# Who asks for the down weights of an expert round: SyncE's queue or ScalarE's

## The chip, the core and the metric

The kernel runs on one core of one Trainium2 chip. The metric is the device time of one execution in microseconds (us). Three executions of the kernel before took 2102.54, 2100.34 and 2096.74 us; the median is 2100.34 us.

## What is computed

A trunk of two layers on 1024 tokens of 1024 channels in float32: a token mixer (layer 0 a gated one, layer 1 a pooling one), and after each a mixture of experts. In the mixture a router picks two of 32 experts for each token, and each expert is a gated pair of matrices and a down matrix:

```
def expert_block(args):
    xb, e = args                                   # 128 token rows, one expert
    hid = jax.nn.silu(xb @ w_gate[e]) * (xb @ w_up[e])   # 1024 -> 512
    return hid @ w_down[e]                               # 512 -> 1024
```

2048 pairs of a token and an expert are cut into blocks of at most 128 rows of one expert. The results go back to their tokens, weighted and added.

## The kernel before

**Items and rounds.** One block of one expert is an item. There are n items in a layer (n is found on the device, and every engine reads it from a small table in SBUF). Round i computes gate and up of item i (on TensorE: 8 weight chunks of 128 x 1024, the helper `gate_up`), then transposes the rows of item i+1 (`x_transposes`, line 850), then down of item i-1 (4 chunks, `down`), then transposes item i's hidden rows (line 888). So a round eats 12 chunks of 512 KB: units 0 to 7 (gate and up, `GU`) and 8 to 11 (down, `DN`).

**How a chunk gets to TensorE.** It lands in one of 12 raw slots (8 in `big`, 4 in `raw`; `moe_raw`). ScalarE rounds it into `w_hi` (`unit`, recorded at line 1025), VectorE subtracts that from the raw chunk into `w_lo` (line 1420), and TensorE multiplies three times for each pair of tiles (hi x hi, hi x lo, lo x hi: lines 619 to 621). `w_hi` and `w_lo` are rings of 4 slots: ScalarE may write the `w_hi` slot of a unit only when TensorE is done with the unit four before (the wait on `M.used` in `unit`, line 1227). VectorE waits for `M.hi`, TensorE for `M.lo`. `M.lo` also tells that the raw slot is free, since VectorE reads it last.

**ScalarE's round** (`round_`, lines 1261 to 1272): units 0 to 3, two copies of the finished rows out of PSUM (`y_out`, line 1248), the split of the hidden rows (`h_split`), units 4 to 7, SiLU (line 1240), units 8 to 11, and at the end the split of the next item's rows, two copies (`x_split`). VectorE's round follows it: units 0 to 3, `h_split`, units 4 to 11, the product `hidden` (line 1792), `x_split`. ScalarE, VectorE, TensorE, GpSimd and SyncE each have a loop of their own over the rounds, with an index register; ScalarE's loop starts at line 1308.

**Who asks for the chunks.** SyncE, on its DMA queue, in a loop over i from 4 to n-1 (lines 403 to 411): it reads two expert numbers from the table, then for j = 0 to 7 waits until unit j of round i-1 is through VectorE and asks for gate or up chunk j of item i (`load_gu`, recorded at line 341), then for j = 0 to 3 waits for unit 8+j of round i-1 and asks for down chunk j of item i-1 (`load_dn`, line 345), which round i uses. After the loop SyncE asks for the last item's four down chunks into other slots (lines 412 to 414), and in layer 0 for weights of the next stage (lines 417 to 420). GpSimd gathers and scatters the token rows on a queue of its own.

The lines on which the change works:

```
with sp.Fori(4, n) as i:                       # 403
    e_up = sp.value_load(table[... i ...])     # 404
    e_dn = sp.value_load(table[... i - 1 ...]) # 405
    for j in range(GU):                        # 406
        sp.wait_ge(M.lo, ROUND * (i - 1) + j + 1)
        load_gu(e_up, j)
    for j in range(DN):                        # 409
        sp.wait_ge(M.lo, ROUND * (i - 1) + GU + j + 1)
        load_dn(e_dn, j)
```

Of the kernel before, what the change touches and what calls it, by code (L numbers as in the profile page):

```python
# [18 lines left out]
P = 128  # L19
# [10 lines left out]
E = 32  # L30
# [6 lines left out]
GU, DN = 8, 4  # L37
ROUND = GU + DN
# [24 lines left out]
def encoder_trunk(nc, A, out):  # L63
    ctx = ExitStack()
    with ctx:
        def sb(name, shape, dt):
            return ctx.enter_context(nc.sbuf_tensor(name, shape, dt))
# [30 lines left out]
        table = sb("table", [1, 2, TABLE], I32)  # L98
# [60 lines left out]
        moe_raw = [bu[:, n * UNIT:(n + 1) * UNIT] for n in range(GU)] + [raw[:, n, :] for n in range(DN)]  # L159
# [114 lines left out]
        def _(sp):  # L274
# [58 lines left out]
            def moe(L, next_weights):  # L333
                M = m[L]
# [4 lines left out]
                def load_gu(e, j, slots=moe_raw):  # L339
                    w = gate if j < DN else up  # L340
                    sp.dma_start(slots[j].rearrange("p (e k f) -> p e k f", e=1, k=2),
                                 w[:, bass.ds(e, 1), j % DN, :, :]).then_inc(M.raw[j], 16)

                def load_dn(e, j, slot=None, landed=None):
                    sp.dma_start((slot if slot is not None else moe_raw[GU + j]).rearrange("p (e k d) -> p e k d", e=1, k=1),
                                 down[:, bass.ds(e, 1), j:j + 1, :]) \
                        .then_inc(landed if landed is not None else M.raw[GU + j], 16)
# [54 lines left out]
                n = sp.value_load(table[0:1, 0, TABLE - 1:TABLE], min_val=E - 2, max_val=ITEMS_MAX - 2) + 2  # L402
                with sp.Fori(4, n) as i:
                    e_up = sp.value_load(table[0:1, 0, bass.ds(i, 1)], min_val=0, max_val=E - 1)
                    e_dn = sp.value_load(table[0:1, 0, bass.ds(i - 1, 1)], min_val=0, max_val=E - 1)
                    for j in range(GU):
                        sp.wait_ge(M.lo, ROUND * (i - 1) + j + 1)
                        load_gu(e_up, j)
                    for j in range(DN):
                        sp.wait_ge(M.lo, ROUND * (i - 1) + GU + j + 1)  # L410
                        load_dn(e_dn, j)
                e_dn = sp.value_load(table[0:1, 0, bass.ds(n - 1, 1)], min_val=0, max_val=E - 1)
                for j in range(DN):
                    load_dn(e_dn, j, early_raw[j], g.last_dn)
# [32 lines left out]

            sp.sem_inc(q.lo, RING)
            moe(0, pool_first)


# [13 lines left out]
            for hf in range(HALVES):  # L465
                pool_out(hf, HALVES * PV + hf * PO)
            moe(1, lambda n: None)


# [553 lines left out]
        def _(act):  # L1023
# [186 lines left out]
            def moe(L, wait_y, wait_tile):  # L1210

                M, n1 = m[L], 4 * L + 3
# [11 lines left out]
                def unit(c, loads, used, gap=0, slots=moe_raw):  # L1224
                    act.wait_ge(M.raw[c], 16 * loads)
                    if used is not None:
                        act.wait_ge(M.used, used)
                    copy(w_hi[:, c % RING, :], slots[c]).then_inc(M.hi, 1 + gap)

                def x_split(i, dst=x_hi):  # L1230
                    for b in range(2):
                        act.wait_ge(M.x_full, 2 * i + b + 1)
                        copy(dst[:, 4 * b:4 * b + 4, :].rearrange("p k t -> p (k t)"), bank[4 + b][:, :]) \
                            .then_inc(M.x_hi, 1)

                def silu(i):
                    act.wait_ge(M.used, ROUND * i + DN)
                    if L == 0 and isinstance(i, int) and i == 0:
                        act.wait_ge(g.fold_stored, 16 * 2)
                    nc.scalar.activation(silu_g, bank[0][:, :], ACT.Silu).then_inc(M.silu, 1)  # L1240

                def h_split(i, dst=h_hi):
                    act.wait_ge(M.h_full, i + 1)
                    copy(dst.rearrange("p k t -> p (k t)"), bank[6][:, :]).then_inc(M.h_hi, 1)
# [6 lines left out]
                def y_out(i, used):  # L1251
                    act.wait_ge(M.used, used)
                    act.wait_ge(M.meta_s, i + 1)
                    weighted_rows(y_sb, 2, meta_s)
# [6 lines left out]
                def round_(i, slots, down_slots=moe_raw, following=True):  # L1261
                    for c in range(4):
                        unit(c, i + 1, ROUND * i + c - 3, slots=slots)
                    y_out(i - 2, ROUND * i)
                    h_split(i - 1)
                    for c in range(4, GU):
                        unit(c, i + 1, ROUND * i + c - 3, slots=slots)
                    silu(i)
                    for c in range(GU, ROUND):
                        unit(c, i, ROUND * i + c - 3, slots=down_slots)  # L1270
                    if following:
                        x_split(i + 1)
# [32 lines left out]
                round_(2, moe_raw, early_down)  # L1305
                act.wait_ge(rt.table, L + 1)
                n = act.value_load(table[0:1, 0, TABLE - 1:TABLE], min_val=E - 2, max_val=ITEMS_MAX - 2) + 2
                with act.Fori(3, n - 1) as i:
                    round_(i, moe_raw)
                round_(n - 1, moe_raw, following=False)  # L1310
                end_unit(0, n)
                end_unit(1, n)
# [729 lines left out]
```

## Time and profile before

| what | before |
|---|---|
| median of three executions | 2100.34 us (2096.74 to 2102.54) |
| span of the profiled execution, first to last instruction | 2094.7 us |
| TensorE, busy share of the span | 97% |
| TensorE's granted clock, mean | 0.982 |
| VectorE | 75% |
| ScalarE | 65% |
| DMA, mean over the span | 267 GB/s |
| SyncE's queue (q1), share of 16 engines' span | 64.7% |
| ScalarE's queue (q10) | 1.3% |

Of the profiled execution only the span is recorded, no device time of its own. The median of the three executions stands 5.6 us above that span, the fastest 2.0 us and the slowest 7.8 us. A share is an average over very different stages: the two stages of expert rounds fill about half of the span, and there every engine is far busier than in the rest. So the shares above only say where to look; the rows further down are from one round and from the two stages.

### The profile page before, as it was taken

How to read it: one execution, taken by the hardware profiler on the slowest of the kernel's cores; microseconds unless marked ns; L12 is line 12 of the kernel's file. 1: busy time of each engine (PE TensorE's matmuls, PEld its weight loads, DVE VectorE, ACT ScalarE, POOL GpSimd, SP SyncE). 2: the span in 40 equal slices, each digit the busy share in tenths (PEclk: the TensorE clock that was granted, in tenths of full speed). 3: DMA queues.
4: the chain of work that ended last, by engine and by line, in shares of the span. 5: the costliest groups of instructions: out<-in, count | busy, mean ns of one | idle time of the engine just before them, and what ended most of it. 6: DMA issues, size and time to landing. Idle time of an engine off the chain costs nothing.

```text
span 2094.7 us, 32415 instructions
## 1 busy us (share of the span) xinstructions
PE 2023.5 (97%) x9566; PEld 1677.0 (80%) x9566; DVE 1567.1 (75%) x1878; ACT 1362.9 (65%) x1744; POOL 358.0 (17%) x439
## 2 busy tenths in 40 slices
PE   7999999999998999999999989998799999999996
PEld 6888778888877888888888868887688888888883
DVE  4334453336568999999999986867799999999995
ACT  3452244433447888888888874325588888888884
POOL 1000000000022222222232200001322222222220
PEclk9999999999999999999999989998799999999998
DMA  7232213332459999999999984233889999999996
GB/s 286 92 99 71 82 61 122 102 100 102 160 148 342 357 380 380 388 385 372 383 376 386 393 319 148 91 150 131 275 331 375 382 378 380 376 379 390 392 374 259
DMA packets 166952, 560.15 MB, mean 267 GB/s; under 512 B 31552, under 2 KB 32800, under 8 KB 164848
## 3 DMA queue, kind: packets, MB, share of 16 engines
q1 hardware_dynamic: 138960, 510.72, 64.7%
q0 software_dynamic: 25488, 39.57, 5.5%
q10 hardware_dynamic: 2448, 9.14, 1.3%
q8 instruction: 32, 0.52, 0.1%
q14 instruction: 24, 0.20, 0.0%
HBM read 541.94 MB, written 51.97 MB: 284 GB/s over the span
## 4 chain that ended last, share of the span: by engine, by line
PE 87%; DVE 5%; DMA 5%; ACT 1%; issue 1%; POOL 1%; SPq 0%; POOLq 0%; DVEq 0%; ACTq 0%
PE bank L619 27%; PE bank L621 26%; PE bank L620 26%; PE bank L850 3%; PE bank L699 1%; PE bank L888 1%; DVE big L1428 1%; DMA big<-in_w_up 1%; PE bank L688 1%; DVE big L1678 1%; DVE bank L1674 1%; DMA raw<-in_w_down 1%; DMA big<-normed,metas 1%; PE bank L738 1%; DMA big<-y_rows 1%
## 5 line engine op out<-in xcount | busy, mean ns | idle before, releaser
L619 PE MATMUL bank<-w_hi,a_hi 128*128 128x512 f32 x1944 | 773.1, 398 | 5.1 <-DVE a_lo L1420 2.8
L621 PE MATMUL bank<-w_hi,a_lo 128*128 128x512 f32 x1944 | 760.5, 391 | 0.0
L620 PE MATMUL bank<-w_lo,a_hi 128*128 128x512 f32 x1944 | 758.4, 390 | 0.0
L1420 DVE TENSOR_TENSOR w_lo<-raw,w_hi 128x1024 fp32r<-128x1024 f32 x372 | 454.2, 1225 | 353.4 <-ACT w_hi L1025 328.9
L1025 ACT ACTIVATE w_hi<-raw 128x1024 fp32r<-128x1024 f32 x372 | 392.8, 1060 | 458.2 <-PE bank L621 435.3
L1420 DVE TENSOR_TENSOR w_lo<-big,w_hi 128x1024 fp32r<-128x1024 f32 x530 | 620.1, 1219 | 29.3 <-ACT w_hi L1025 23.7
L1025 ACT ACTIVATE w_hi<-big 128x1024 fp32r<-128x1024 f32 x530 | 549.2, 1063 | 107.1 <-PE bank L621 106.9
L619 PEld LDWEIGHTS bank<-w_hi,a_hi 128*128 128x128 f32 x1944 | 367.1, 189 | 79.5 <-issue 4.2
L621 PEld LDWEIGHTS bank<-w_hi,a_lo 128*128 128x128 f32 x1944 | 366.0, 188 | 79.2
L620 PEld LDWEIGHTS bank<-w_lo,a_hi 128*128 128x128 f32 x1944 | 366.9, 189 | 72.6
L1420 DVE TENSOR_TENSOR a_lo<-bank,a_hi 128x512 fp32r<-128x512 f32 x227 | 147.7, 683 | 39.2 <-ACT a_hi L1025 39.2
L619 PE MATMUL bank<-a_hi,w_hi 128*128 128x512 f32 x384 | 149.7, 390 | 0.0
L621 PE MATMUL bank<-a_hi,w_lo 128*128 128x512 f32 x384 | 149.4, 389 | 0.0
L620 PE MATMUL bank<-a_lo,w_hi 128*128 128x512 f32 x384 | 149.4, 389 | 0.0
L1025 ACT ACTIVATE a_hi<-bank 128x512 fp32r<-128x512 f32 x227 | 125.3, 595 | 36.4 <-PE bank L850 23.8
L570 POOL DMA_INDIRECT y_rows<-big,metas x65 | 66.6, 1024 | 317.6 <-ACT big L1248 303.0
L619 PE MATMUL bank<-w_hi,y_hi 128*128 128x512 f32 x256 | 101.3, 396 | 5.3 <-DVE big L1678 3.6
L621 PE MATMUL bank<-w_hi,y_lo 128*128 128x512 f32 x256 | 100.1, 391 | 0.0
L620 PE MATMUL bank<-w_lo,y_hi 128*128 128x512 f32 x256 | 100.1, 391 | 0.0
L554 POOL COPY metas<-cols 128x4 int32<-128x4 int32 x61 | 65.4, 1072 | 159.7 <-PE bank L850 135.6
L850 PEld LDWEIGHTS bank<-cf,big 128*128 128x128 f32 x520 | 73.4, 206 | 21.4 <-DMA big<-normed,metas 12.4
L850 PE MATMUL bank<-cf,big 128*128 128x128 f32 x520 | 74.4, 287 | 15.8 <-DMA big<-normed,metas 15.8
(199 smaller groups left out, 1707.0 us busy)
## 6 DMA issues: line engine op xcount, KB each, us to landing
big<-in_w_gate SPq DMA_DIRECT2D x260, 512.0 KB, 5.3
big<-in_w_up SPq DMA_DIRECT2D x254, 512.0 KB, 5.7
raw<-in_w_down SPq DMA_DIRECT2D x244, 512.0 KB, 5.7
raw<-in_a_w_in SPq DMA_DIRECT2D x64, 512.0 KB, 3.9
raw<-in_a_w_out SPq DMA_DIRECT2D x32, 512.0 KB, 3.3
big<-y_rows SPq DMA_DIRECT2D x12, 1024.0 KB, 7.4
big<-in_w_down SPq DMA_DIRECT2D x16, 512.0 KB, 7.9
raw<-in_b_w_in SPq DMA_DIRECT2D x16, 512.0 KB, 5.0
```

The source lines that it names most:

```text
L554: nc.gpsimd.tensor_copy(meta_g, ahead_g).then_inc(M.meta_g, 1)
L570: pool.indirect_dma_start(out=y_rows[L][:, :], out_offset=bass.IndirectOffsetOnAxis(ap=meta[:, 1:2], axis=0), in_=rows.rearrange("p n f -> ...
L619: pe.matmul(dst, left_hi, right_hi, start=first, stop=False)
L620: pe.matmul(dst, left_hi, right_lo, start=False, stop=False)
L621: return pe.matmul(dst, left_lo, right_hi, start=False, stop=last)
L688: last = pe.transpose(bank[b + k // 4][:, k % 4 * P:(k % 4 + 1) * P], x_res[:, t, k * P:(k + 1) * P], ident)
L699: last = pe.matmul(bank[b][:, 0:LGC], xt[L][t][:, k * P:(k + 1) * P], router[:, k, :], start=k == 0, stop=k == KC - 1)
L738: last = pe.matmul(bank[c % nb][:, t * P:(t + 1) * P], v_all[:, t, c * P:(c + 1) * P], w_s[:, c * P * HEADS // SGU, :], start=True, stop=True)
L850: last = pe.transpose(bank[4 + k // 4][:, k % 4 * P:(k % 4 + 1) * P], rows[:, k // 2, k % 2, :], ident)
L888: last = pe.transpose(bank[6][:, k * P:(k + 1) * P], cols_of[:, k, :], ident)
L1025: return nc.scalar.activation(dst, src, ACT.Copy)
L1420: return nc.vector.tensor_tensor(dst, src, f32(hi), ALU.subtract)
```

## The change

SyncE's loop loses the read of the second expert number and the four waits and requests for down chunks. ScalarE's loop gets them, behind the whole of its round: at the end of round i it reads the expert number of item i from the table, and for j = 0 to 3 waits until unit 8+j of round i is through VectorE and asks, on ScalarE's own DMA queue, for down chunk j of item i. Slots, sizes, semaphores and the set of transfers are the same. The loops' bounds cover the same items (before: i-1 from 3 to n-2 on SyncE; after: i from 3 to n-2 on ScalarE).

```
                 with sp.Fori(4, n) as i:
                     e_up = sp.value_load(table[0:1, 0, bass.ds(i, 1)], min_val=0, max_val=E - 1)
-                    e_dn = sp.value_load(table[0:1, 0, bass.ds(i - 1, 1)], min_val=0, max_val=E - 1)
                     for j in range(GU):
                         sp.wait_ge(M.lo, ROUND * (i - 1) + j + 1)
                         load_gu(e_up, j)
-                    for j in range(DN):
-                        sp.wait_ge(M.lo, ROUND * (i - 1) + GU + j + 1)
-                        load_dn(e_dn, j)
...
+                down_of = A["w_down"][L].rearrange("e (k p) d -> p e k d", p=P)
                 with act.Fori(3, n - 1) as i:
                     round_(i, moe_raw)
+                    e_dn = act.value_load(table[0:1, 0, bass.ds(i, 1)], min_val=0, max_val=E - 1)
+                    for j in range(DN):
+                        act.wait_ge(M.lo, ROUND * i + GU + j + 1)
+                        act.dma_start(moe_raw[GU + j].rearrange("p (e k d) -> p e k d", e=1, k=1),
+                                      down_of[:, bass.ds(e_dn, 1), j:j + 1, :]).then_inc(M.raw[GU + j], 16)
                 round_(n - 1, moe_raw, following=False)
```

## Rows read from the trace of the kernel before

**Rows 1.** Both stages of expert rounds: busy time, granted clock, DMA share, GB/s.
```profile
core 0: us, PE busy (x) PEld busy (x) DVE busy (x) ACT busy (x) POOL busy (x), PEclk, DMA share, GB/s
680.94:1196.75 515.81, 515.81 (x2436) 430.74 (x2435) 482.43 (x465) 446.66 (x522) 141.70 (x174) 1.00 0.98 380
1527.00:2025.00 498.00, 498.00 (x2352) 415.86 (x2351) 465.88 (x448) 430.98 (x505) 136.10 (x167) 1.00 0.98 378
```

**Rows 2.** Waits in layer 0's rounds, 688.5 to 1192.3 us (none is TensorE's).
```profile
ACT w_hi L1025 <- PE bank L621: 67.6, 226, 0.4
...
DVE a_lo L1420 <- ACT a_hi L1025: 12.1, 29, 0.4
DVE w_lo L1420 <- ACT w_hi L1025: 7.5, 29, 0.3
```

**Rows 3.** Timeline, ScalarE, from unit 11 of one round to unit 10 of the next.
```profile
start us, us, engine line op out<-in xcount [idle before <-releaser]
1105.81 1.06 ACT L1025 ACTIVATE w_hi<-raw 128x1024 fp32r<-128x1024 f32 x1 [0.30 <-PE bank L621]
1106.77 1.07 ACT L1025 ACTIVATE a_hi<-bank 128x512 fp32r<-128x512 f32 x2
1108.13 1.06 ACT L1025 ACTIVATE w_hi<-big 128x1024 fp32r<-128x1024 f32 x1 [0.29 <-PE bank L621]
...
1112.30 1.06 ACT L1025 ACTIVATE w_hi<-big 128x1024 fp32r<-128x1024 f32 x1 [0.36 <-PE bank L621]
...
1114.88 2.97 ACT L1025 ACTIVATE w_hi<-big 128x1024 fp32r<-128x1024 f32 x3
...
1119.59 1.05 ACT L1025 ACTIVATE w_hi<-raw 128x1024 fp32r<-128x1024 f32 x1
1120.86 1.06 ACT L1025 ACTIVATE w_hi<-raw 128x1024 fp32r<-128x1024 f32 x1 [0.23 <-PE bank L621]
1122.22 1.06 ACT L1025 ACTIVATE w_hi<-raw 128x1024 fp32r<-128x1024 f32 x1 [0.30 <-PE bank L621]
```

**Rows 4.** Timeline, VectorE, the same round.
```profile
1105.54 2.58 DVE L1420 TENSOR_TENSOR w_lo<-raw,w_hi 128x1024 fp32r<-128x1024 f32 x2
...
1109.84 4.78 DVE L1420 TENSOR_TENSOR w_lo<-big,w_hi 128x1024 fp32r<-128x1024 f32 x4
```

**Rows 5.** Timeline, TensorE: transposes, down, gate and up, the next round's transposes.
```profile
1105.61 1.11 PE L850 MATMUL bank<-cf,big 128*128 128x128 f32 x8
1106.47 0.47 PE L619 MATMUL bank<-w_hi,a_hi 128*128 128x512 f32 x1
...
1112.39 0.47 PE L619 MATMUL bank<-w_hi,a_hi 128*128 128x512 f32 x1
...
1123.40 1.11 PE L850 MATMUL bank<-cf,big 128*128 128x128 f32 x8
```

**Rows 6.** ScalarE's loop branch: all rounds, then one round; line 1227 behind it.
```profile
L1308 ACTq COMPARE_BRANCH  x57: 40/45/54, 697.4 to 2026.7; - x57
...
L1308 ACTq FUSED_REGOPS  x2: 37/44/50, 1106.8 to 1107.0; - x2
...
L1227 ACTq FUSED_REGOPS  x1: 37/37/37, 1107.1 to 1107.1; - x1
```

**Rows 7.** SyncE's table read and four requests; a wait's sum; ScalarE's table read.
```profile
L412 SPq FUSED_REGOPS  x2: 51/102/152, 1197.8 to 1198.2; - x2
L412 SPq TENSOR_LOAD <-table x1: 276/276/276, 1197.9 to 1197.9; - x1
L412 SPq SEQ_ASSERT  x1: 18/18/18, 1198.4 to 1198.4; - x1
...
L345 SPq FUSED_REGOPS  x4: 37/37/37, 1198.5 to 1200.0; - x4
L345 SPq MOVE big<-in_w_down x4: 29/29/29, 1198.6 to 1200.1; - x4
L345 SPq DMA_DIRECT2D big<-in_w_down x4: 332/332/333, 1198.6 to 1200.2; - x4
...
L410 SPq ALU_OP  x2: 37/37/37, 1105.9 to 1107.3; - x2
...
L1307 ACTq TENSOR_LOAD <-table x1: 466/466/466, 679.6 to 679.6; - x1
```

**Rows 8.** DMA requests on ScalarE's queue: one beside a running activation; the first one.
```profile
554.28 1.06 ACT L1025 ACTIVATE w_hi<-raw 128x1024 fp32r<-128x1024 f32 x1 [2.91 <-PE bank L621]
554.30 0.40 ACTq L1063 DMA_DIRECT2D normed<-big  x1
...
L1119 ACTq DMA_DIRECT2D cf<-in_c_float x1: 432/432/432, 0.9 to 0.9; - x1
```

**Rows 9.** TensorE released by VectorE, across engines.
```profile
1214.84 0.68 DVE L1792 TENSOR_TENSOR big<-bank,big 128x512 f32<-128x512 f32 x1
...
1215.58 0.33 PE L888 MATMUL bank<-cf,big 128*128 128x128 f32 x1 [0.29 <-DVE big L1792]
```

**Rows 10.** SyncE's requests in one round; landing of down chunks, 1100 to 1220 us.
```profile
1111.22 3.89 SPq L341 DMA_DIRECT2D big<-in_w_gate  x4
1117.24 3.74 SPq L341 DMA_DIRECT2D big<-in_w_up  x4
1122.07 4.34 SPq L345 DMA_DIRECT2D raw<-in_w_down  x4
...
DMA to landing us min/median/max: 5.1/5.8/9.2
```

**Rows 11.** TensorE's waits for transfers, whole kernel.
```profile
PE bank L1000 <- DMA big<-y_rows: 5.9, 1, 5.9
...
PE bank L1000 <- DMA raw<-y_rows: 1.0, 1, 1.0
```

**Rows 12.** Two windows inside a round, busiest and barest; columns as in the first group.
```profile
1105.70:1107.20 1.50, 1.50 (x12) 1.42 (x11) 1.36 (x2) 1.40 (x2) 0.16 (x1) 1.00 1.03 418
...
1119.20:1120.70 1.50, 1.50 (x9) 1.23 (x8) 1.45 (x3) 1.44 (x3) 0.00 (x0) 1.00 0.93 348
```

## The prediction

> **What bounds the kernel now.** I read the stages first: in the two stretches of expert rounds TensorE is busy for the whole of 515.81 and 498.00 us at a granted clock of 1.00 (the 2.4 GHz level), VectorE for 94% and ScalarE for 87% [rows 1]. Then the waits of these rounds: TensorE has none, ScalarE waits for TensorE 226 times (67.6 us in 504 us), always to refill the ring of four, and VectorE waits for ScalarE twice a round, for 0.4 and 0.3 us [rows 2]. So the rounds run at TensorE's pace, 17.79 us each (1105.61 to 1123.40, [rows 5]), and neither a transfer nor a queue holds them: nothing can be gained in them, and the question is whether the new work on ScalarE's sequencer stays under TensorE's cover. For that I read one round instruction by instruction on the three engines [rows 3 to 5].
>
> **What the change removes.** SyncE loses a table read and four requests a round. Its gate and up requests still wait for VectorE to free each slot (first request at 1111.22, [rows 10]), so they go out when they did. Worth: nothing.
>
> **What it adds on ScalarE, and when.** ScalarE's sequencer runs ahead of its engine by one pending activation: the loop branch stands at 1106.8, when the first of the two row copies starts at 1106.77 and the second is still to run [rows 3, 6]. The new instructions take the place of that branch, so they begin at 1106.8 and run beside the two copies. That a request runs beside an activation is in the trace: a 0.40 us request at 554.30 inside an activation of 554.28 to 555.34 [rows 8]. The table read: SyncE's, instruction by instruction, 0.051 + 0.276 + 0.152 + 0.018 = 0.50 us, with four gaps of 0.04, 0.66 us (from 1197.8 to 1198.5, [rows 7]). A request: 0.037 + 0.029 + 0.333 with three gaps of 0.04 is 0.52 us, which is the spacing of the four there (1198.6 to 1200.2 for three); the sum for the wait's value adds 0.037 and a gap, so 0.59 us, and four are 2.37 us. The waits themselves: unit 11 goes into VectorE when ScalarE is done with it (1105.81 + 1.06 = 1106.87) and is through at about 1108.12 (1105.54 + 2.58, [rows 4]); the fourth request gets to its wait at about 1106.76 + 0.66 + 3 x 0.59 = 1109.2. So no wait blocks. The last request ends at 1106.76 + 0.66 + 2.37 = 1109.79. The branch and the first wait's sum follow, 0.32 us before (1106.8 to 1107.1, [rows 6]) and 0.08 for the sum itself: ScalarE starts unit 0 of the next round at **1110.19** in place of 1108.13 [rows 3], 2.06 us later.
>
> **What is queued behind it.** Unit 0 is needed by TensorE when gate and up begin; down (24 products) and four transposes lie between, so that is at 1112.37, just ahead of the row at 1112.39 [rows 5]. After its start it takes 1.06 us on ScalarE, 0.03 to VectorE, 1.21 there (4.78 us for four, overlapping a little, [rows 4]) and 0.05 from VectorE's end to TensorE (1214.84 + 0.68 to 1215.58, [rows 9]): 2.36 us. 1110.19 + 2.36 = 1112.55 against 1112.37: TensorE waits 0.18 us. Before, the same unit was ready at 1109.84 + 1.21 + 0.05 = 1111.10, with 1.27 us in hand, and VectorE came to it 0.65 us after ScalarE was done (1109.84 for 1109.19): that cover eats all but a tenth of the 2.06 us. Units 1 to 3 follow at 0.97 us each in place of TensorE's pace, so unit 3 starts at 1113.10 against 1112.30, and y_out, h_split and unit 4 are 0.80 us late. Unit 4 then starts at 1115.68; 1.06 + 0.03 + 1.21 + 0.05 gives 1118.03, where TensorE comes at 1112.37 + 4 x 1.36 = 1117.81, or 1117.99 with the 0.18 (TensorE's time for one unit, by which it spaces ScalarE's units at 1120.86 and 1122.22, [rows 3]): 0.04 more. By unit 9 ScalarE waits for TensorE again: unit 8 at about 1120.0 for 1119.59, unit 9 at 1121.05, which is 1120.86 with TensorE's own delay; VectorE, with 94% busy, gets back to ScalarE's heels by unit 11. So nothing piles up from round to round; what is lost is what TensorE waited, **0.22 us a round**. ScalarE's loop turns 57 times [rows 6]: 57 x 0.22 = 12.5 us. In the same measure: span 2094.7 + 12.5 = 2107.2 us, and the median stands 5.6 us above the span shown, so 2100.3 + 12.5, about 2113, which I round down to 2112 since the gaps are more likely over- than undercounted in 0.04 steps.
>
> **The bounds of that cost.** ScalarE's trace shows no request or table read inside a round. Below: if the sum for the wait costs nothing beside the rest (4 x 0.077 less), the last request ends at 1109.48 and TensorE never waits: 0 us. Above: a request as long as ScalarE's first, 0.432 us [rows 8], adds 0.4, and a table read as long as ScalarE's one so far, 0.466 us [rows 7], adds 0.19: 0.22 + 0.59 = 0.81 us a round, 46 us. I take SyncE's figures because they are the same instructions in a running loop; the first of a kind on an engine is the far row. The Trainium skill (DMA: Bandwidth & Descriptors, Latency and other measured facts) gives a tensor load a floor of about 600 ns. The trace disagrees, with 276 ns for the load alone; by the page the table read would cost 0.32 us more and the change 31 us in all.
>
> **The transfers.** Down chunk 0 is asked for at about 1107.6 in place of 1104.3 (the round before its row at 1122.07, [rows 10]), chunk 3 at 1109.3 in place of 1108.3. Unit 8 reads the first at 1120.0. That is 12.4 us for a landing that took 5.8, 9.2 at most [rows 10]: hidden. SyncE's requests end at 1121 and ScalarE's begin at 1125.3, a pause of 4.4 us that the transfers in flight (5.8 us each to land) about fill; the queues move 380 GB/s on average [rows 1] and 418 at best [rows 12], so 9% of a round, 1.6 us, may stand idle before transfers bind. After the loop SyncE asks for the last down chunks and the next stage's weights some 5 us earlier, while ScalarE's last four wait in their own queue; they have the same 12 us. Nothing.
>
> **The rivals.** *It is hidden after all* (not slower). For it: the shortfall is 0.2 us out of 3.0, and rests on gaps of 0.04 us. It decides at a unit 0 that starts by 1110.0, that is, when table read and requests take less than 2.83 us in place of 3.03. Time 2100, give or take 2. The Trainium skill (DMA: Bandwidth & Descriptors, Issuing engines are not separate DMA queues) says that issuing on several engines only saves sequencer time, and here SyncE's was never short; by that rule this case holds. *The sequencer's work is dearer on ScalarE*: 0.5 to 0.81 us a round, 2129 to 2147. It sits in the same place and decides from requests of 0.40 us each. For it: ScalarE's own first request and read [rows 7, 8]; against: they were the first of their kind. The Trainium skill's floor for a tensor load (same page and section as above) would put the read's share of it at the upper end; no row shows it in a loop. *The transfers fall behind*: if more than 1.6 us a round stood idle, each further 1 us would cost 57 us, 2157; against: 12 us of cover. *Faster*: not in the rounds, as TensorE is full there; only at the ends, where loads go out earlier, and there TensorE's waits for transfers after the rounds are 5.9 + 1.0 us [rows 11], on rows that wait for the scatter and not for weights: 2093 at best.
>
> **How the numbers follow.** Chances: the forecast (0.1 to 0.5 us a round, 2106 to 2129) 0.45; hidden 0.40; dearer 0.09; transfers behind 0.02; faster 0.04. What can be told from no change is 0.3%, 6.3 us, or 0.11 us a round. Slower is 0.45 + 0.09 + 0.02 = 0.56, same 0.40, faster 0.04. The range takes in the hidden case and its scatter (2097) and goes into the dearer one to 0.54 us a round (2131). The likeliest case's own range is 2106 to 2129.
>
> **What would show it.** Right: in the rounds TensorE shows a wait for VectorE's w_lo (line 1420) once a round at the start of gate and up, of about 0.2 us, and rounds of 18.0 us; ScalarE's unit 0 starts 2.0 us later after the second row copy, with units 1 to 3 spaced by 0.97 us; VectorE waits for w_hi at unit 0 for about 1.1 us. Hidden: the same shifts, but no wait of TensorE and 17.79 us. Dearer: requests over 0.4 us or a table load over 0.4 us, and a wait of TensorE of 0.5 us or more. Wrong altogether: rounds longer with ScalarE waiting for a landing of a down chunk, or requests that hold until the activations before them are done, so that unit 0 starts after 1110.5.

## The result, and the profile after

The changed kernel takes **2113.7 us** (median of four runs, 2108.7 to 2117.3), where the kernel before took 2099.3 us in the four runs beside it: slower, at a ratio of 1.0075 (95%: 1.0061 to 1.0089), some 13 to 19 us. The forecast of 2112 us was close. Part of that is luck: two causes of different size add up to it, and the smaller one stood in the prediction at nothing.

All times below are of profiled executions unless a median is named. The one of the changed kernel was the fastest of its four, at 2108.7 us; what the other three lost on top, no trace shows. Its span grew from 2094.7 to 2107.0 us, by 12.3. Measured from one round's row transposes on TensorE to the next, each of the 57 looped rounds took 17.80 us before (17.79 and 17.81 by turns, [rows 5]) and 18.03 us on average after (17.79 to 18.91). That is 13.2 us over all rounds; outside them the changed kernel gained 0.9. The first looped round of each layer begins before the first request on ScalarE and still takes 17.79 us, so it is 55 rounds that carry the loss, 0.24 us each.

The window view over layer 0's rounds in the changed kernel, for the first line of [rows 1] (window, length, busy us of TensorE, its weight loads, VectorE, ScalarE and GpSimd, granted clock, DMA share, GB/s):

```profile
690.00:1195.00 505.00, 504.16 (x2357) 416.89 (x2357) 457.20 (x449) 418.35 (x505) 119.22 (x168) 1.00 0.99 376
```

The clock is still 1.00 (2.4 GHz). TensorE seems as full as before, while VectorE and ScalarE are down from 94% and 87% to 91% and 83%. The rounds' 1.3% are a part of that; the rest is overlap, since instructions that follow one another at once, as units 0 to 3 below, take 3.91 us for four where one alone takes 1.06.

The waits of layer 0's rounds in the changed kernel, which answer to [rows 2] (columns: us in total, times, longest):

```profile
ACT w_hi L1021 <- PE bank L617: 73.4, 81, 2.5
DVE w_lo L1422 <- ACT w_hi L1021: 45.3, 67, 1.6
...
ACT w_hi L1021 <- DMA raw<-in_w_down: 9.3, 11, 1.8
...
PEld bank L615 <- DVE w_lo L1422: 3.4, 13, 0.8
...
PE bank L615 <- DVE w_lo L1422: 0.6, 1, 0.6
```

Three things are to be seen. ScalarE's 226 short waits for its ring have become 81 long ones: it now comes late once a round instead of waiting at each unit. ScalarE waits 11 times for a down chunk to land, which it never did before. And TensorE's own row holds a single wait of 0.6 us, its weight loads another 13 of 3.4 us in all, though 28 of these rounds are longer, by 5.8 us together: most delays of 0.1 to 0.2 us do not show there, and have to be read from start times.

One ordinary round, on the three engines (start, duration):

```profile
732.64 1.07 ACT L1021 ACTIVATE a_hi<-bank 128x512 fp32r<-128x512 f32 x2
733.44 2.13 ACTq L1310 DMA_DIRECT2D raw<-in_w_down  x4
736.00 3.91 ACT L1021 ACTIVATE w_hi<-big 128x1024 fp32r<-128x1024 f32 x4 [2.30 <-PE bank L617]
```

```profile
737.10 3.50 DVE L1422 TENSOR_TENSOR w_lo<-big,w_hi 128x1024 fp32r<-128x1024 f32 x3 [1.31 <-ACT w_hi L1021]
```

```profile
737.91 0.60 PE L884 MATMUL bank<-cf,big 128*128 128x128 f32 x4
738.38 0.50 PE L615 MATMUL bank<-w_hi,a_hi 128*128 128x512 f32 x1
```

This round began at 731.47. The second row copy starts 1.64 us later, at 733.11, as in the kernel before; the four requests stand in the place of the branch of [rows 6], and unit 0 starts at 736.00: 4.53 us into the round, where it was 2.52 before (1108.13 - 1105.61, [rows 3, 5]). It ends at 737.06, VectorE starts on it at 737.10 with no cover left, is done about 1.21 later at 738.31, and TensorE's first gate/up product follows at 738.38. That is 0.47 us behind the transposes of h, where it was 0.35 before (1112.04, then 1112.39), and 6.91 us into the round for 6.79. In layer 0's rounds before, this product came at 6.79 throughout. "PE bank L617" in the bracket of unit 0 names the last semaphore that unit 0 waited for; ScalarE's own requests are what held it up.

Two rounds in which the last down chunk (unit 11) is late, ScalarE alone. The first begins at 1127.65, the second at 1036.70:

```profile
1126.47 1.06 ACT L1021 ACTIVATE w_hi<-raw 128x1024 fp32r<-128x1024 f32 x1 [0.30 <-PE bank L617]
1128.18 1.06 ACT L1021 ACTIVATE w_hi<-raw 128x1024 fp32r<-128x1024 f32 x1 [0.64 <-DMA raw<-in_w_down]
1129.14 0.58 ACT L1021 ACTIVATE a_hi<-bank 128x512 fp32r<-128x512 f32 x1
1129.62 0.36 ACTq L1310 DMA_DIRECT2D raw<-in_w_down  x1
1129.62 0.59 ACT L1021 ACTIVATE a_hi<-bank 128x512 fp32r<-128x512 f32 x1
1130.20 1.61 ACTq L1310 DMA_DIRECT2D raw<-in_w_down  x3
1132.24 3.91 ACT L1021 ACTIVATE w_hi<-big 128x1024 fp32r<-128x1024 f32 x4 [2.02 <-PE bank L617]
```

```profile
1038.35 1.06 ACT L1021 ACTIVATE w_hi<-raw 128x1024 fp32r<-128x1024 f32 x1 [1.75 <-DMA raw<-in_w_down]
1039.32 0.58 ACT L1021 ACTIVATE a_hi<-bank 128x512 fp32r<-128x512 f32 x1
1039.37 0.36 ACTq L1310 DMA_DIRECT2D raw<-in_w_down  x1
1039.80 0.59 ACT L1021 ACTIVATE a_hi<-bank 128x512 fp32r<-128x512 f32 x1
1039.95 1.54 ACTq L1310 DMA_DIRECT2D raw<-in_w_down  x3
```

In the first, unit 11 waits 0.64 us for its down chunk and the row copies behind it are late, but the requests are not: the first goes out 1.97 us into the round (1129.62), as in the ordinary one (733.44 for 731.47). Unit 0 starts at 4.59 because the second request took 0.47 us. In the second, unit 11 waits 1.75 us, the first request goes out only 2.67 us into the round, unit 0 starts at 5.22 (1041.92), and the round takes 18.68 us. The page of the profile shows where the late chunks come from, in its section of transfers (count, KB each, median us from request to landing):

```profile
big<-in_w_gate SPq DMA_DIRECT2D x260, 512.0 KB, 9.0
big<-in_w_up SPq DMA_DIRECT2D x254, 512.0 KB, 10.0
raw<-in_w_down ACTq DMA_DIRECT2D x228, 512.0 KB, 9.1
```

Before, the same three medians were 5.3, 5.7 and 5.7 us.

Laid side by side, the 55 rounds follow two simple sums. The first instruction of the table read starts at the later of two moments, to 0.01 us: 1.15 us into the round, when TensorE has just ended the second four of the row transposes, for which the second row copy waits, and 0.21 us behind the start of unit 11. In 27 rounds unit 11 waits for its chunk, but in only 8 does it start late enough to move the read, and in two of these by no more than 0.07 us. And a round takes 17.80 us plus the start of unit 0 less 4.37 us, to within 0.05 us.

### The profile page after: what moved, and what is told of

It reads as the page before. It is cut to its first block, busy times and chain, and to the rows that moved or that the text cites. A ratio compares the mean times of both kernels' runs of the same rounds, so it can differ in the third digit from the quotient of the medians.

```text
span 2107.0 us, 32418 instructions
## 1 busy us (share of the span) xinstructions
PE 2033.4 (97%) x9566; PEld 1676.1 (80%) x9566; DVE 1548.1 (73%) x1878; ACT 1334.9 (63%) x1745; POOL 320.0 (15%) x439
## 4 chain that ended last, share of the span: by engine, by line
PE 70%; DMA 19%; DVE 5%; issue 2%; ACTq 2%; ACT 2%; POOL 1%; SPq 0%; POOLq 0%; DVEq 0%
PE bank L615 21%; PE bank L617 21%; PE bank L616 21%; DMA raw<-in_w_down 15%; PE bank L846 2%; PE bank L695 1%; ACTq L1310 1%; DVE big L1430 1%; DMA lists<-payload,place 1%; PE bank L884 1%; POOL lists L524 1%; DMA big<-normed,metas 1%; PE bank L684 1%; DVE big L1680 1%; DVE bank L1676 1%
## 5 line engine op out<-in xcount | busy, mean ns | idle before, releaser
L617 PE MATMUL bank<-w_hi,a_lo 128*128 128x512 f32 x1944 | 760.6, 391 | 0.0
L1422 DVE TENSOR_TENSOR w_lo<-raw,w_hi 128x1024 fp32r<-128x1024 f32 x372 | 444.7, 1222 | 357.0 <-ACT w_hi L1021 351.5
L1422 DVE TENSOR_TENSOR w_lo<-big,w_hi 128x1024 fp32r<-128x1024 f32 x530 | 615.7, 1220 | 83.3 <-ACT w_hi L1021 81.7
L1021 ACT ACTIVATE w_hi<-big 128x1024 fp32r<-128x1024 f32 x530 | 521.9, 1055 | 136.6 <-PE bank L617 126.2
L615 PEld LDWEIGHTS bank<-w_hi,a_hi 128*128 128x128 f32 x1944 | 366.8, 189 | 95.9 <-DVE w_lo L1422 12.4
L617 PEld LDWEIGHTS bank<-w_hi,a_lo 128*128 128x128 f32 x1944 | 366.1, 188 | 79.3
L617 PE MATMUL bank<-a_hi,w_lo 128*128 128x512 f32 x384 | 149.6, 390 | 0.0
L617 PE MATMUL bank<-w_hi,y_lo 128*128 128x512 f32 x256 | 100.6, 393 | 0.0
L559 POOL COPY metas<-cols 128x4 int32<-128x4 int32 x63 | 22.3, 354 | 424.3 <-DMA cols<-lists 424.3
```

Source lines behind the costliest of these rows:

```text
L559: nc.gpsimd.tensor_copy(meta_s, ahead_s).then_inc(M.meta_s, 1)
L615: pe.matmul(dst, left_hi, right_hi, start=first, stop=False)
L617: return pe.matmul(dst, left_lo, right_hi, start=False, stop=last)
L1021: return nc.scalar.activation(dst, src, ACT.Copy)
L1422: return nc.vector.tensor_tensor(dst, src, f32(hi), ALU.subtract)
```

## The experiments

Two theories went into them. **S**: ScalarE's sequencer is what costs, with its table read and four requests between the second row copy and unit 0. **T**: the requests for the down chunks come late and in a burst after a pause, the DMA engines run short, and chunks land late.

| kernel | median us | ratio to before, 95% | span | excess of the 57 rounds over 17.80 |
|---|---|---|---|---|
| after | 2113.7 | 1.0061 to 1.0089 | 2107.0 | 13.2 |
| e1_sync_late | 2112.2 | 1.0045 to 1.0089 | 2109.2 | 5.2 |
| e2_read_early | 2106.5 | 1.0029 to 1.0063 | 2104.6 | 6.1 |
| e3_read_twice | 2136.2 | 1.0174 to 1.0208 | 2134.1 | 37.7 |
| e4_spread | 2096.1 | 0.9993 to 1.0012 | 2094.3 | 0 |
| e5_small_requests | 2097.8 | 0.9992 to 1.0011 | 2099.5 | 0 |
| e6_small_full | 2098.3 | 1.0001 to 1.0020 | 2096.4 | 2.0 |
| e7_small_read_twice | 2126.9 | 1.0131 to 1.0165 | 2124.4 | 30.7 |
| e8_sync_pairs | 2095.7 | 0.9988 to 1.0009 | 2091.6 | 0 |
| e9_filled_pause | 2117.4 | 1.0076 to 1.0109 | 2115.6 | 18.5 |
| e10_sync_late_filled | 2120.3 | 1.0090 to 1.0131 | 2117.6 | 12.9 |
| e11_one_held | 2114.9 | 1.0060 to 1.0094 | 2114.1 | 14.6 |
| e12_sync_late_one_held | 2113.2 | 1.0045 to 1.0084 | 2115.0 | 6.9 |

Each kernel's ratio is to the kernel before on the same chip; its medians there were 2096.4 to 2099.3 us (one execution of 10643 us beside e4 and e6 to e8 is left out of the ratios).

### The late burst without ScalarE (e1), the read moved away (e2), the read doubled (e3)

e1 is the kernel before, with one wait ahead of SyncE's four requests:

```
+                    sp.wait_ge(M.lo, ROUND * (i - 1) + GU + DN)
                     for j in range(DN):
-                        sp.wait_ge(M.lo, ROUND * (i - 1) + GU + j + 1)
                         load_dn(e_dn, j)
```

> SyncE keeps the down requests, but waits once for unit 11 to be through VectorE and then asks for all four: the times of the changed kernel's requests (2.7 to 4.2 us after the rows' transposes begin, against 2.0 to 4.0) without anything new on ScalarE. Theory S (the time ScalarE's sequencer needs between the second row copy and unit 0 sets the loss): TensorE never waits, rounds of 17.80 us, 2099 us, even if chunks land later. Theory T (the late burst of requests makes chunks land late, and that sets the loss): down chunks land after 9 us or more, ScalarE waits for some of them, 2103 to 2113 us.

It lost 14 us by the ratio, with nothing new on ScalarE's sequencer. So T is real, against the prediction. But it lost them in another way than the changed kernel. The first 22 rounds of layer 0 take 17.79 or 17.81 us as before; after them single rounds take 0.1 to 0.6 more; and of the 14.5 us by which its span is longer only 5.2 are in the looped rounds. From the end of one layer's looped rounds to the start of the other's it takes 336.8 us, where the kernels whose landings stay short (before, e4 to e8) take 330.6 to 333.1, and behind the second layer's rounds 72.4, where they take 69.2 to 70.0. That late chunks hold up what follows there is likely, but was not followed up. The rest, 1.8 us, lies ahead of the loops, where nothing was changed and those kernels differ among themselves by 5 us. The median landing of a down chunk grows under it. In the window 690 to 800 us, and then in 1020 to 1110 us, in e1:

```profile
raw<-in_w_down SPq DMA_DIRECT2D x24, 512.0 KB, 6.7
...
raw<-in_w_down SPq DMA_DIRECT2D x20, 512.0 KB, 12.5
```

In the changed kernel:

```profile
raw<-in_w_down ACTq DMA_DIRECT2D x24, 512.0 KB, 6.5
...
raw<-in_w_down ACTq DMA_DIRECT2D x20, 512.0 KB, 10.4
```

In the kernel before both windows have a median of 5.5 and 5.4.

e2 is the changed kernel with the table read in another place, behind ScalarE's unit 8:

```
                     for c in range(GU, ROUND):
                         unit(c, i, ROUND * i + c - 3, slots=down_slots)
+                        if read and c == GU:
+                            e_dn = act.value_load(table[0:1, 0, bass.ds(i, 1)], ...)
...
                 with act.Fori(3, n - 1) as i:
-                    round_(i, moe_raw)
-                    e_dn = act.value_load(table[0:1, 0, bass.ds(i, 1)], ...)
+                    e_dn = round_(i, moe_raw, read=True)
```

> The changed kernel with the table read moved up, behind unit 8 of the round, where ScalarE's sequencer is a unit ahead; the four waits and requests stay at the end. Theory S: unit 0 starts 0.66 us earlier than in the changed kernel, about 3.9 us after the rows' transposes begin in place of 4.54; the shortfall was 0.23 us, so TensorE stops waiting and the time is 2099 to 2102 us. Theory T: the requests go out only 0.66 us earlier, still in one burst, so chunks land late as before and the time stays at 2107 to 2113 us.

Unit 0 starts 4.01 us into the round on average, for 4.62 in the changed kernel, and the first gate/up product is back at 6.79 us: the sequencer's cost is gone. Yet 9.7 us by the ratio are left, and 6.1 us of its profile are in single rounds later on, with ScalarE waiting for transfers, as here in layer 0's rounds:

```profile
ACT w_hi L1021 <- DMA big<-in_w_up: 16.1, 13, 2.3
...
ACT w_hi L1021 <- DMA raw<-in_w_down: 6.0, 10, 1.3
```

That is T by itself again, now through ScalarE's queue.

e3 doubles the read in the changed kernel:

```
                     e_dn = act.value_load(table[0:1, 0, bass.ds(i, 1)], ...)
+                    e_dn = act.value_load(table[0:1, 0, bass.ds(i, 1)], ...)
```

> The changed kernel with the table read done twice at its place. Theory S: with the cover used up, every further 0.66 us on ScalarE's sequencer is paid in full in each of the 57 rounds: 38 us more than the changed kernel, 2151 us, rounds of 18.7 us. Theory T: requests 0.66 us later each round; as the transfers in flight fill most of that, 2114 to 2125 us.

The rounds take 18.46 us, 0.66 over 17.80, and 0.43 more than the changed kernel's mean. The second read delays unit 0 by 0.43 us (5.05 for 4.62, means), and the rounds grow by the same. That is less than the 38 us more that S gave: a second read takes 0.54 us, not 0.66 (first request at 2.52 us into the round for 1.98), and the rounds with a late chunk are gone. Now the waits show on TensorE as well:

```profile
PEld bank L615 <- DVE w_lo L1423: 38.0, 60, 1.2
...
PE bank L615 <- DVE w_lo L1423: 22.8, 58, 0.8
```

Once the cover is used up, what is added to the sequencer is paid in full, once a round. And T all but disappears: in e3 the median landing stays at 6.2 and 6.3 us in the same two windows, and unit 11 never waits for a chunk. A round of 18.46 us leaves the DMA engines nearly 4% more time for the same bytes, which would explain it; no run tests that alone. S and T do not simply add.

### ScalarE's work with the transfers on time (e5, e6, e7); other ways to ask (e4, e8)

e5 leaves SyncE's requests of the kernel before as they are, and puts on ScalarE, at the change's place, a table read, four waits that are met, and four requests of 16 partitions x 16 bytes into an unused corner of a tile (`small_of`, `spare` and `base` are set ahead of the loop):

```
                 with act.Fori(3, n - 1) as i:
                     round_(i, moe_raw)
+                    e_dn = act.value_load(table[0:1, 0, bass.ds(i, 1)], ...)
+                    for j in range(DN):
+                        act.wait_ge(spare[j], 16 * i + base - 48)
+                        act.dma_start(cols[0:16, 8 + 4 * j:12 + 4 * j]..., small_of[0:16, bass.ds(e_dn, 1), j:j + 1, 0:4])...
```

> The kernel before (SyncE asks for the down chunks as ever), and on ScalarE, at the place of the change, a table read, four waits that are met, and four requests of 16 partitions x 16 bytes into a free corner of cols. The sequencer's work without the moved transfers. Theory S: what the changed kernel loses in rounds whose chunks land in time, 0.16 us a round, to all of its 0.23: 2108 to 2112 us. Theory T: 2099 us, since no transfer that matters has moved. Requests this small may take another time on the sequencer than 0.34 us.

Not one round is longer, where theory S had 2108 to 2112 us: as it stood, this spoke against S. But unit 0 starts earlier here than in the changed kernel. Its four waits share one computed sum, so it has three sums fewer than the change; e6 gives each its own (`base - 48 + j`), and e7 is e6 with the read done twice.

> As e5_small_requests, with a sum of its own for each of the four waits, as in the changed kernel (3 x 0.07 us more on ScalarE's sequencer). Unit 0 then starts 4.36 us after the rows' transposes begin; TensorE needs it by 4.43. Theory S with these figures: 0 to 0.03 us a round, 2098 to 2100 us, VectorE's w_lo 0 ready less than 0.15 us ahead of TensorE. If more than 2103 us, the sequencer alone explains more than I now think.

> As e6_small_full with the table read done twice: the sequencer is 0.62 us longer, the transfers stay at SyncE's times. Theory S: unit 0 starts at 4.98, TensorE waits 0.55 us a round, 57 x 0.55 = 31 us, 2129 us, as e3_read_twice lost 38 us with its larger requests. Theory T alone: 2098 us.

e6 loses 2.0 us in its rounds (most take 17.83 to 17.87, none over 17.95), e7 30.7. Unit 0 starts 4.20 us into the round in e5, 4.40 in e6 and 4.93 in e7 (means). With the same 2.36 us from unit 0 to TensorE as in the prediction, 6.79 - 2.36 = 4.43 is where TensorE's first gate/up product begins to be late; measured by whole rounds the edge is the 4.37 us of above, and it is the same in e3, e6 and e7. The runs lie around it as they should: e5 loses nothing, e6 0.04 us a round, and e7's further 0.53 us of delay cost 0.52. So S holds as a mechanism, with its edge within 0.06 us of where it was put. But e6 stops just at that edge, and the changed kernel's ordinary rounds, with unit 0 at 4.54, are 0.14 us beyond e6, because its requests of 512 KB take the sequencer longer than the tiny ones. All of e6's, then all of the changed kernel's (min/median/max ns):

```profile
L1317 ACTq DMA_DIRECT2D cols<-in_w_down x228: 322/323/428, 698.3 to 2030.2; - x114
```

```profile
L1310 ACTq DMA_DIRECT2D raw<-in_w_down x228: 339/340/601, 697.5 to 2040.7; - x114
```

The four means of a round add up to 1.45 us in the changed kernel and 1.31 in e6, and the starts are 0.58 to 0.62 us apart for 0.55 to 0.57. Size as such is the lesser part of it, 0.34 for 0.32 us at the median. The rest are single requests, mostly the second of the four, that take up to 0.60 us; in e4 (below), where requests of the same size go out one by one, the mean is 0.342 us and the longest 0.377. Why they take longer in the changed kernel's burst stays open.

e4 keeps the requests on ScalarE's queue, but issues the first three beside a running activation and all near the time at which VectorE frees their slots: the read behind unit 8, chunk 0 behind unit 10, chunk 1 behind unit 11, chunks 2 and 3 behind the row copies (`ask_down` is the wait and the request of one chunk).

```
                         unit(c, i, ROUND * i + c - 3, slots=down_slots)
+                        if ask and c == GU:
+                            e_dn = act.value_load(table[0:1, 0, bass.ds(i, 1)], ...)
+                        if ask and c >= GU + 2:
+                            ask_down(i, e_dn, c - GU - 2)
                     if following:
                         x_split(i + 1)
+                    if ask:
+                        ask_down(i, e_dn, 2)
+                        ask_down(i, e_dn, 3)
```

> ScalarE still asks for the down chunks on its own queue, but at SyncE's old times and under running activations: the table read behind unit 8, request 0 behind unit 10, request 1 behind unit 11, requests 2 and 3 behind the row copies. Both theories: nothing is lost, 2096 to 2100 us; down chunks land in under 7 us, rounds of 17.80 us. If the queue itself (ScalarE's in place of SyncE's) made the difference, it would stay near 2107 to 2114 us.

e8 is the kernel before, with SyncE asking for the down chunks in two pairs, each after its second slot is free (`if j % 2 == 0: sp.wait_ge(M.lo, ROUND * (i - 1) + GU + j + 2)`).

> SyncE asks for the down chunks in two pairs, when unit 9 and when unit 11 are through VectorE, so the pause in the requests is 2.4 and 2.2 us in place of the 5 us of e1_sync_late. Theory T in the form that the DMA engines run dry in the pause and have no room to catch up: with this pause the transfers in flight cover it; landings stay under 8 us, 2097 to 2101 us. If any burst costs, whatever the pause: half of e1_sync_late's loss, 2105 us.

Neither loses anything. ScalarE in e4, in one round that begins at 1106.60:

```profile
1105.43 1.06 ACT L1021 ACTIVATE w_hi<-raw 128x1024 fp32r<-128x1024 f32 x1 [0.30 <-PE bank L617]
1105.64 0.35 ACTq L1261 DMA_DIRECT2D raw<-in_w_down  x1
1106.79 1.06 ACT L1021 ACTIVATE w_hi<-raw 128x1024 fp32r<-128x1024 f32 x1 [0.30 <-PE bank L617]
1107.00 0.34 ACTq L1261 DMA_DIRECT2D raw<-in_w_down  x1
1107.76 0.58 ACT L1021 ACTIVATE a_hi<-bank 128x512 fp32r<-128x512 f32 x1
1107.94 0.34 ACTq L1261 DMA_DIRECT2D raw<-in_w_down  x1
1108.23 0.59 ACT L1021 ACTIVATE a_hi<-bank 128x512 fp32r<-128x512 f32 x1
1109.27 0.34 ACTq L1261 DMA_DIRECT2D raw<-in_w_down  x1
1110.04 2.96 ACT L1021 ACTIVATE w_hi<-big 128x1024 fp32r<-128x1024 f32 x3 [1.21 <-DVE w_lo L1430]
```

The fourth request does not lie beside an activation: it waits until VectorE is through unit 11 and runs at 1109.27, when the row copies are over. It delays unit 0 to 3.44 us into the round, from 2.53, and that costs nothing because it is short of 4.37. So ScalarE's queue is no worse than SyncE's, and four requests and a read a round on ScalarE are free if they go out on time and lie beside activations or, where they don't, leave unit 0 ahead of the edge. What the change costs, it costs by where it puts them.

With these the requests' times can be set beside the load of the DMA engines, in the seventh round of layer 0, 2 to 4 us after its start. The windows are of before, e4, e8, the changed kernel and e1, in that order, with the rest of the round too for before and the changed kernel (the last two columns: DMA share, GB/s; in windows this short the share can come out above 1):

```profile
733.80:735.80 2.00, 2.00 (x11) 1.63 (x10) 2.00 (x4) 1.38 (x3) 1.14 (x2) 1.00 1.02 418
...
739.80:749.60 9.80, 9.80 (x44) 8.08 (x43) 8.85 (x9) 8.89 (x11) 1.95 (x3) 1.00 0.93 346
```

```profile
734.78:736.78 2.00, 2.00 (x11) 1.62 (x10) 2.00 (x4) 0.79 (x2) 1.14 (x2) 1.00 1.02 350
```

```profile
732.22:734.22 2.00, 2.00 (x11) 1.63 (x10) 2.00 (x4) 1.38 (x3) 1.14 (x2) 1.00 1.01 387
```

```profile
733.47:735.47 2.00, 2.00 (x11) 1.62 (x10) 2.00 (x4) 0.23 (x1) 1.14 (x2) 1.00 0.81 289
735.47:739.47 4.00, 4.00 (x21) 3.24 (x20) 2.69 (x4) 3.47 (x4) 1.06 (x2) 1.00 0.81 295
739.47:749.27 9.80, 9.80 (x45) 8.06 (x44) 9.60 (x9) 9.40 (x12) 1.56 (x2) 1.00 1.02 391
```

```profile
735.64:737.64 2.00, 2.00 (x11) 1.63 (x10) 2.00 (x4) 1.38 (x3) 1.14 (x2) 1.00 0.61 207
```

Down chunk 0 is asked for 1.3 us ahead of the round's start in before (730.47 for 731.80), 1.0 ahead in e4, at the start in e8, and 2.0 and 2.7 us behind it in the changed kernel and e1. The first three have their engines at 1.01 or more, the other two at 0.81 and 0.61, though the rates of the first three differ (350 to 418 GB/s). The other lines of the first and the fourth fence show why it is hardly made up for: in the last 9.8 us of the round the changed kernel's engines are at 1.02, where before's stood at 0.93. What is missed early falls to a stretch that has 9% left, and the backlog comes back as longer landings. Six rounds later the dip is nearly gone, which fits with requests that are still outstanding in the pause; the landings are what has grown. The changed kernel's round that begins at 839.04, the same two windows:

```profile
841.04:843.04 2.00, 2.00 (x11) 1.63 (x10) 2.00 (x4) 0.23 (x1) 1.14 (x2) 1.00 0.96 346
843.04:847.04 4.00, 4.00 (x21) 3.31 (x20) 2.76 (x4) 3.54 (x4) 1.06 (x2) 1.00 1.01 390
```

The last of the four down chunks decides when a round is hit: it is asked for 3.8 us into a round and read by unit 11 14.4 us later, and its landing takes 14 to 15.7 us in most of layer 0's later rounds.

### Closing the pause instead (e9 to e12)

If the dry stretch alone were the cause, holding back one or two up requests, so that they fill the pause ahead of the down requests, should cure it. e9 is the changed kernel with the last two up requests held until VectorE is through units 9 and 11; e10 is e1 with the same; e11 and e12 hold only the last up request, until unit 9.

```
                     for j in range(GU):
-                        sp.wait_ge(M.lo, ROUND * (i - 1) + j + 1)
+                        sp.wait_ge(M.lo, ROUND * (i - 1) + (GU + 2 * j - 10 if j > 5 else j + 1))
```

> The changed kernel, all of it, but SyncE holds back the last two up requests of each round until units 9 and 11 are through VectorE, so that requests go on while ScalarE has not yet asked. ScalarE's sequencer has the same work, with requests of 512 KB; the DMA engines no longer run dry. What is left is theory S with the real requests: unit 0 at 4.40 to 4.48 us against 4.43, 0.03 to 0.1 us a round, 2099 to 2104 us, and down chunks land in under 8 us. If the dry pause had no part in the changed kernel's loss: 2109 to 2114 us.

> e1_sync_late with the same two up requests held back. The four down requests still go out late and in one burst, from SyncE. Theory T (the pause is the cause): landings stay at 6 to 8 us, 2096 to 2100 us. If the burst or the lateness itself cost: 2105 to 2112 us, as e1_sync_late.

> e9_filled_pause held two requests and so only moved the pause (4.6 us now behind the sixth). Here the changed kernel, with only the last up request held, until unit 9 is through VectorE: requests at 14.6, 17.8 and 20.0 us of the round, no pause over 3.2 us. Theory T: the DMA engines stay fed, down chunks land in under 8 us all through a stage. What is left is the sequencer with requests of 512 KB: unit 0 at 4.44 us, TensorE waits about 0.1 us a round, 2102 to 2107 us. If lateness alone and not the pause made landings grow: 2109 to 2118 us, landings of 9 us and more.

> e1_sync_late (SyncE asks for all four down chunks after unit 11, ScalarE has nothing new) with the same one up request held until unit 9: pauses of 3.7 and 2.9 us in place of 5.5. Theory T: landings grow far less than in e1_sync_late, 2096 to 2103 us. If the late burst costs whatever the pause: 2109 to 2115 us.

None cured anything, and e10 is worse than what it should mend, by intervals that just do not overlap (2120.3 for 2112.2), e9 if anything (2117.4 for 2113.7). e9's windows say why: it moved the pause rather than closed it. Its seventh round begins with these two:

```profile
733.65:735.65 2.00, 2.00 (x14) 1.82 (x13) 1.86 (x2) 1.80 (x3) 0.56 (x1) 1.00 0.78 246
735.65:737.65 2.00, 2.00 (x11) 1.63 (x10) 2.00 (x4) 0.23 (x1) 1.14 (x2) 1.00 0.82 254
```

The changed kernel was at 1.03 in the first of them. In e10 the down requests also went out 0.4 us later than in e1 (3.08 us into the round for 2.69), so it changed two things at once. e12 raised e1's 0.61 to 0.79 in the same place and won nothing. One thing the early rounds of the changed kernel and of e11 do show: long before unit 11 has to wait for a chunk, they already take 17.86 to 18.02 us and 17.95 to 18.25. That is the sequencer's part without late landings.

## Why the prediction was right in its number, and where it was wrong

**The sequencer, right in place and nearly in size.** Forecast: table read and requests begin with the first row copy, unit 0 comes 2.06 us later, VectorE and TensorE have 1.27 us in hand and 0.65 more of VectorE's, TensorE waits 0.18 us at gate and up and 0.04 at unit 4. Measured, in the round at 731.47: table load from 732.69 on, with the first copy at 732.64; first request at 733.44, the last over at 735.57, unit 0 0.43 us behind that (forecast 0.40). In the 28 rounds whose unit 11 does not wait for its chunk: unit 0 2.01 us later than before; the first gate/up product 0.12 us later; the whole round 0.17 longer, for 0.22. Over 55 rounds that is some 9 us in place of 12.5. ScalarE's table load took what SyncE's had:

```profile
L1307 ACTq TENSOR_LOAD <-table x57: 274/278/303, 696.7 to 2038.2; - x57
```

The bound by ScalarE's first load of 466 ns [rows 7] was the far one, and the Trainium skill's floor of about 600 ns for a tensor load (DMA: Bandwidth & Descriptors, Latency and other measured facts) is not met here either. Units 0 to 3 follow one another without a gap (3.91 us for four, as forecast 0.97 each), and VectorE waits 1.31 us at unit 0 for a forecast of about 1.1. e5, e6 and e7 confirm the edge, e3 the slope. The sign for it was badly chosen: a wait of 0.2 us a round was to show on TensorE and mostly doesn't, in the waits; it shows in the starts.

**The start of the read, right by coincidence.** "ScalarE's sequencer runs ahead of its engine by one pending activation" was read from a branch at 1106.8 beside a row copy at 1106.77. The late rounds refute it: in the one at 1036.70 the read begins at 1038.56, 0.76 us ahead of the first row copy (1039.32), with both copies still pending. What holds the read is the wait of the second copy for TensorE's transposes (1105.61 + 1.15 is 1106.76 as well) and, in late rounds, the landing for which unit 11 waits. In an ordinary round both readings give the same time, so the sum came out right. The prediction's 5.6 us between median and span were not an overhead either: in every run with both on record the time is 1.6 to 1.7 us above its own span.

**The transfers, wrong.** They stood at "Nothing", as a rival at 0.02, and they cost some 4 of the 13.2 us. In 27 rounds unit 11 waits for its chunk, and these cost 0.32 us each in place of 0.17: 27 x 0.15 = 4.1 us of the 13.2. Most of it, 3.4 us, is in only six of them (at 1036.70 and five in layer 1), in which the wait is so long that the table read and the requests start late; they take 18.17 to 18.91 us. The other 21 cost 0.20 us, hardly more than an ordinary round. The prediction had named the sign, "rounds longer with ScalarE waiting for a landing of a down chunk", under "wrong altogether". Alone, T is larger still: e1 loses 14 us and e2 9.7. That they don't add up to more in the changed kernel fits with e3: every 0.17 us by which the sequencer lengthens a round is time for the DMA engines to catch up. This is argued, not tested. So the failed step is the one in two halves on the pause. "A pause of 4.4 us that the transfers in flight about fill": the pause was 3.9 us (725.79 + 3.74 to 733.44), and the engines' share fell to 0.81 in the six microseconds behind it. And "9% of a round, 1.6 us, may stand idle before transfers bind", from 380 against 418 GB/s: by the share of busy time the slack is smaller. It was 0.98 on average [rows 1] and 1.03 at best [rows 12], 5% or 0.9 us a round, and (1.03 - 0.81) x 6 us is 1.3 us that the changed kernel left idle in its seventh round. Both are estimates. The 12.4 us of cover were there (14.4 us for the last chunk), but were compared with landings of the kernel before (5.8, at most 9.2); the landings themselves moved, to a median of 10.4 and a maximum of 15.7 in 1020 to 1110 us, after thirteen rounds in which no wait for a chunk could be seen, only the longer landings.

**The rivals.** "Hidden": wrong; its condition, unit 0 at 1110.0 at the latest, 4.4 us into the round, is where e6 stands, and e6 is nearly hidden. "Dearer on ScalarE": wrong in size; a 512 KB request took 0.36 us on average and up to 0.60, for 0.34 of SyncE's requests for down chunks in the kernel before and of ScalarE's own in e4. "Issuing on several engines only saves sequencer time" (the Trainium skill, DMA: Bandwidth & Descriptors, Issuing engines are not separate DMA queues): for the queue as such the runs agree, as e4 costs and wins nothing; what it leaves out is that the new sequencer's time may be on the path. "Faster": nothing of it; the 0.9 us outside the rounds is within what can't be told, as the stretch ahead of the loops alone varies by 5 us.

**What stays open.** How much of T is the dry stretch and how much the lateness of the burst as such. e1 and the changed kernel have both, e4 and e8 neither, and the attempts to separate them (e9 to e12) put a pause or a squeeze elsewhere. That T is 4 us of the changed kernel's loss rests on sorting the rounds of its one profile, its fastest execution, by whether unit 11 waits for its chunk, and not on a run. The runs show that S and T are each there. T alone is enough to make the kernel slower (e1, e2); S alone was tested with tiny requests, where it costs 0.1% (e6), and with the read doubled (e7), but not at the changed kernel's own size.

## What to carry to other kernels

An engine that refills a ring hides a request of its own beside a running activation, or as far as the next consumer is covered; here, at the end of the loop's body, a read and four requests delayed unit 0 by 2.01 us where about 1.84 (4.37 - 2.53) were covered. When the DMA engines are at 0.98 of their time, a request has to go out when its slot comes free, by whichever queue: later ones cost nothing for 12 to 22 rounds in e1, e10 and e12 while landings grow, and then stall the engine that reads them, so look at the landing time by stretches and not only at waits. Sum up the slack of a transfer stage by the share of busy time too, and not only by the best GB/s in a window: here the first gave 0.9 us and the second 1.6, for a pause that left 1.3 us idle.

## What the runs showed of the hardware that was not expected

- A request takes ScalarE's sequencer longer when it moves more: 0.323 us at the median for 16 partitions x 16 bytes, 0.340 for 512 KB, with single ones to 0.60. The mean of the latter was 0.36 in the changed kernel's burst and 0.34 one by one (e4).
- A transfer of 256 bytes in all, asked for in the midst of the weights' traffic, took 4.7 us to land at the median (4.3 to 5.3), nearly as long as 512 KB (5.7) in the kernel before.
- Landings can double, 5.7 to over 10 us, and for 12 to 22 rounds not one round gets longer by a hundredth of a microsecond (e1, e10, e12).
- Short delays of TensorE are hardly in its waits: of 5.8 us in layer 0's rounds, its own row holds 0.6 us and that of its weight loads 3.4; the round at 731.47, 0.12 us late at its first gate/up product, shows none.
- ScalarE's sequencer works at least two pending activations ahead of its engine: the table read at 1038.56 came before the row copies at 1039.32 and 1039.80.
